# First item of the expert stage: rows fetched, copied and turned in the router's block; its bias row loaded by SyncE

## The reference, cut to what matters

```python
x = layer_norm(DEEPNORM_ALPHA * x + mix_out, ln1_g, ln1_b)
logits = x2d @ w_router + b_router
top_vals, top_idx = lax.top_k(logits, 4); gates = softmax(top_vals)
# for each expert e and its tokens:
gu = xb @ w_gate_up[e] + b_gate_up[e]          # 1024 -> 2048
hid = (clip(u, -7, 7) + 1) * (g * sigmoid(1.702 * g))   # g = min(g, 7)
y += gate * (hid @ w_down[e] + b_down[e])      # 1024 -> 1024
x = layer_norm(DEEPNORM_ALPHA * x + y, ln2_g, ln2_b)
```

## Time and profile before

| | us |
|---|---|
| median of 3 runs | 1393.29 |
| lowest, highest | 1393.19, 1395.59 |
| the profiled execution, whole | 1394.65 |
| its span | 1392.8 |
| PE busy in the span | 1342.5 (96%) |
| DVE, ACT busy | 467.6, 262.0 |
| mean granted TensorE clock | 0.978 |
| read from HBM | 493.07 MB |

### The profile page before, as it was taken

How to read it: one execution, slowest core, us unless ns; L and a number is a source line. 1 busy time by engine, 2 the same in 40 slices (tenths; PEclk the granted TensorE clock), 3 DMA queues, 4 the chain that set the end, 5 groups by cost and what they waited for, 6 DMA issues and landing times.

```text
span 1392.8 us, 20454 instructions
## 1 busy us (share of the span) xinstructions
PE 1342.5 (96%) x7640; PEld 513.0 (37%) x7641; DVE 467.6 (34%) x954; ACT 262.0 (19%) x613; POOL 78.3 (6%) x87
## 2 busy tenths in 40 slices
PE   8899999989999999999999999999999999999995
PEld 6355445654533333333333333333333233333331
DVE  0244456655732222322223222223222322322225
ACT  1333337734320100111001101001110000111002
POOL 2022235300000000000000000000000000000000
PEclk9999999979999999999999999999999899999998
DMA  9559689794368999999999996999999999999991
GB/s 357 223 195 352 238 329 392 309 363 163 121 243 356 416 417 418 418 419 418 417 417 418 418 418 242 378 419 419 418 417 417 417 366 419 420 418 418 416 416 64
DMA packets 96630, 497.91 MB, mean 357 GB/s; under 512 B 9821, under 2 KB 10205, under 8 KB 61770
## 3 DMA queue, kind: packets, MB, share of 16 engines
q1 hardware_dynamic: 84930, 429.91, 76.4%
q0 software_dynamic: 11520, 67.11, 12.3%
q10 hardware_dynamic: 136, 0.28, 0.1%
HBM read 493.07 MB, written 3.93 MB: 357 GB/s over the span
## 4 chain that ended last, share of the span: by engine, by line
PE 64%; DMA 4%; SPq 3%; DVE 1%; issue 1%; ACT 0%; ACTq 0%; DVEq 0%
PE psum L2016 29%; PE psum L2052 15%; PE psum L1986 7%; PE psum L1463 7%; DMA arena<-in_w_gate_up 4%; SPq L268 3%; PE psum L1995 2%; PE psum L1962 1%; PE psum L2040 1%; PE psum L2073 1%; DVE arena L2237 0%; DVE arena L2260 0%; PE psum L1977 0%; DVE arena L2251 0%; ACTq L2094 0%
## 5 line engine op out<-in xcount | busy, mean ns | idle before, releaser
L2016 PE MATMUL psum<-arena 128*64 128x512 f32 x2112 | 469.2, 596 | 4.9 <-DMA arena<-in_w_gate_up 2.7
L2157 DVE SCALAR_TENSOR_TENSOR arena<-psum,arena 64x512 f32<-64x512 f32 (+1 forms) x128 | 126.8, 1010 | 449.9 <-PE psum L1986 449.9
L2016 PEld LDWEIGHTS psum<-arena 128*64 128x64 f32 x2112 | 148.4, 137 | 316.4 <-issue 306.2
L2052 PE MATMUL psum<-arena 128*64 128x512 f32 x1056 | 235.4, 598 | 0.7 <-ACT arena L2119 0.7
L2052 PEld LDWEIGHTS psum<-arena 128*64 128x64 f32 x1056 | 73.2, 137 | 160.0 <-issue 133.1
L2101 ACT ACTIVATE arena<-psum 128x512 f32<-128x512 f32 x34 | 20.3, 598 | 504.1 <-PE psum L1962 504.1
L1986 PE MATMUL psum<-arena 64*128 64x512 f32 (+1 forms) x396 | 109.7, 632 | 0.9 <-ACT arena L2123 0.9
L1463 PE MATMUL psum<-arena 128*64 128x512 f32 (+1 forms) x420 | 103.0, 608 | 1.0 <-ACT arena L2101 0.7
L2189 DVE TENSOR_SCALAR arena<-psum 128x512 f32<-128x512 f32 x33 | 22.8, 692 | 239.4 <-PE psum L2016 239.4
L1193 DVE STREAM_TRANSPOSE arena<-arena 128x1024 f32<-128x1024 f32 x64 | 74.9, 1214 | 1.8 <-DVE arena L1297 1.1
L580 PE MATMUL psum<-arena 128*128 128x512 f32 x128 | 63.8, 631 | 3.7 <-DVE arena L1182 3.7
(11 more groups left out here) (252 smaller groups left out, 994.1 us busy)
## 6 DMA issues: line engine op xcount, KB each, us to landing
arena<-in_w_gate_up SPq DMA_DIRECT2D x256, 1024.0 KB, 15.7
arena<-in_w_down SPq DMA_DIRECT2D x128, 1024.0 KB, 13.0
arena<-in_w_in SPq DMA_DIRECT2D x12, 1024.0 KB, 9.7
arena<-in_w_out SPq DMA_DIRECT2D x4, 1024.0 KB, 9.7
out<-arena SPq DMA_DIRECT2D x12, 256.0 KB, 2.1
arena<-in_x_prompt SPq DMA_DIRECT2D x4, 512.0 KB, 5.1
arena<-in_b_gate_up ACTq DMA_DIRECT2D x68, 4.0 KB
arena<-in_ln_g SPq DMA_DIRECT2D x2, 512.0 KB, 5.8
```

Of the source, the lines that this page charges most:

```text
L2016: ins = nc.tensor.matmul(psum[64 * h:64 * h + 64, n, :], x_k, slot[k][:, col:col + 512], start=False, stop=(k == KD - 1))
L2052: ins = nc.tensor.matmul(psum[64 * h:64 * h + 64, 4, :], h_k, slot[s][:, col:col + 512], start=(k == 0), stop=(k == KD - 1))
L2157: ins = nc.vector.scalar_tensor_tensor(out=r, in0=psum[0:nt, banks[h]:banks[h] + at_once, :], scalar=item_gate[0:nt, b, col], in1=r, op0=A ...
```

## The change

Item 0's steps are moved from the head of the expert block to the end of the router's block. The fetch is made in three pieces in the order (2, 0, 1), the first two behind `rows_ready` 4, the third behind 6. The bias row of expert 0 is loaded by SP, behind the down weights and behind `r_ready` 6 (its place in memory is that of `x_again`, block 1). PE adds it after the last `rank` and runs four warming matmuls there, not six. `ones_rows` is set by DVE after `pick(2)`. The two warming matmuls at the head of the expert block are gone. Item 0 waits for the constant 16, and `extras` is read after item 0.

```diff
@@ router's block, SP
                     load_weights(sp, 0, s)
+                sp.wait_ge(r_ready, 6)
+                for n in range(2):
+                    sp.dma_start(bias_row[32 * n:32 * n + 1, :], a["b_gate_up"][0, 0:1, n * D:n * D + D]).then_inc(bias_loaded, 16)
@@ router's block, PE
                 ins.then_inc(ranked, 1)
-                keep_warm(6)
+                pe.wait_ge(ones_ready, 1)
+                pe.wait_ge(bias_loaded, 32)
+                add_bias()
+                keep_warm(4)
 
                 pe.wait_ge(pick_ready, 3)
+                pe.wait_ge(rows_ready, 4)
+                fetch_block(order[0], first=True, last=False)
+                fetch_block(order[1], first=False, last=False)
                 pe.wait_ge(rows_ready, 6)
-                fetch_rows(0)
+                fetch_block(order[2], first=False, last=True).then_inc(fetched, 1)
                 pe.wait_ge(col_ready, 1)
 ...
+                pe.wait_ge(xg_ready, 1)
+                turn_rows()
@@ router's block, ACT
+                act.wait_ge(fetched, 1)
+                nc.scalar.activation(xg, psum[:, 2, :], ACT.Copy).then_inc(xg_ready, 1)
+                act.wait_ge(xg_turned, 1)
+                nc.scalar.activation(xgT, psum[:, 2, :], ACT.Copy).then_inc(xg_copied, 1)
@@ router's block, DVE
                 pick(2)
+                nc.vector.memset(ones_rows, 1.0).then_inc(ones_ready, 1)
                 off_mean(2, 0)
@@ expert block, all engines
+            body(0, first=True)
             extras = eng.value_load(count_i[0:1, 0:1], min_val=0, max_val=MAX_EXTRA)
-            body(0, first=True)
@@ expert block, PE
-                warm(2)
-                turn(0)
-                pe.wait_ge(ones_ready, 1)
-                pe.wait_ge(ones_ready, 1)
-                add_bias(0)
...
-                    loaded = pe.value_load(started_i[0:1, bass.ds(t, 1)], min_val=16, max_val=16 * EXPERTS)
+                    loaded = 16 if first else pe.value_load(started_i[0:1, bass.ds(t, 1)], min_val=16, max_val=16 * EXPERTS)
@@ expert block, ACT
-                load_bias(0)
-                copy_rows(0)
-                copy_x(0)
@@ expert block, DVE
-                nc.vector.memset(ones_rows, 1.0).then_inc(ones_ready, 1)
```

More of the change, by code:

```diff
@@ L1401, in decoder_step @@
         kept_end = top[0]
+        xg = room(512)
+        xgT = room(512)
+        bias_row = room(D)
+        ones_rows = room(SLOTS)
+        item_end, top[0] = top[0], kept_end
         x_again = room(3 * D).rearrange("p (b d) -> p b d", b=3)
@@ L1437, in decoder_step @@
         ln_loaded = sem("ln_loaded")
+        bias_loaded, xg_turned, xg_copied = sem("bias_loaded"), sem("xg_turned"), sem("xg_copied")
+        bias_used, ones_ready = sem("bias_used"), sem("ones_ready")
         sel_done, pick_ready, fetched, xg_ready = sem("sel_done"), sem("pick_ready"), sem("fetched"), sem("xg_ready")
@@ L1456, in decoder_step, with fetch_block, turn_rows, add_bias @@
         PROJ_BANK = {0: 4, 1: 0}
[L1458 to L1465, removed]
+        def fetch_block(b, first, last):
+            nt = BLOCKS[b][1]
+            for h in range(2):
+                ins = nc.tensor.matmul(psum[64 * h:64 * h + 64, 2, :], pick_rows[0:nt, b, :],
+                                       x1[0:nt, b, h * 512:(h + 1) * 512], start=first, stop=last)
+            return ins
+        def turn_rows():
+            for c in range(4):
+                ins = nc.tensor.transpose(psum[:, 2, c * P:(c + 1) * P], xg[:, c * P:(c + 1) * P], ident)
+            ins.then_inc(xg_turned, 1)
+        def add_bias():
+            for h in range(2):
+                for n in range(2):
+                    ins = nc.tensor.matmul(psum[64 * h:64 * h + 64, n, :], ones_rows[32 * n:32 * n + 1, :],
+                                           bias_row[32 * n:32 * n + 1, h * 512:h * 512 + 512],
+                                           start=True, stop=False)
+            ins.then_inc(bias_used, 1)
         def rows_of_item(dve, t):
@@ L1875, in _ @@
                 links.append(link.n)
[L1878 to L1882, removed]
+        top[0] = item_end
         gate_in, up_in, sig, hid, hidT, y_rows = (room(512) for _ in range(6))
@@ L1892, in decoder_step @@
             sem("base_ready"))
-        bias_loaded, xg_turned, xg_copied = sem("bias_loaded"), sem("xg_turned"), sem("xg_copied")
-        bias_used, hid_ready, hid_turned, hid_copied, y_copied = (
-            sem("bias_used"), sem("hid_ready"), sem("hid_turned"), sem("hid_copied"), sem("y_copied"))
+        hid_ready, hid_turned, hid_copied, y_copied = (
+            sem("hid_ready"), sem("hid_turned"), sem("hid_copied"), sem("y_copied"))
         w_used = [sem(f"w_used{s}") for s in range(RING)]
-        gate_clamped, sig_ready, ones_ready, e_dve = (
-            sem("gate_clamped"), sem("sig_ready"), sem("ones_ready"), sem("e_dve"))
+        gate_clamped, sig_ready, e_dve = (
+            sem("gate_clamped"), sem("sig_ready"), sem("e_dve"))
         base_set, scatter_ready, combined, drained = (
             sem("base_set"), sem("scatter_ready"), sem("combined"), sem("drained"))
-        def warm(n):
-            for _ in range(n):
-                nc.tensor.matmul(psum[:, 7, :], ident, tab[:, 0:BANK], start=True, stop=True)
         def items(eng, body, midway=None):
+            body(0, first=True)
             extras = eng.value_load(count_i[0:1, 0:1], min_val=0, max_val=MAX_EXTRA)
-            body(0, first=True)
             if midway is None:
@@ L1960, in turn @@
                     pe.wait_ge(xg_ready, t + 1)
-                    for c in range(4):
-                        ins = nc.tensor.transpose(psum[:, 2, c * P:(c + 1) * P], xg[:, c * P:(c + 1) * P], ident)
-                    ins.then_inc(xg_turned, 1)
+                    turn_rows()
                 def fetch(t):
                     pe.wait_ge(pick_ready, 3 * t + 3)
-                    fetch_rows(t)
+                    for b in range(3):
+                        ins = fetch_block(b, first=(b == 0), last=(b == 2))
+                    ins.then_inc(fetched, 1)
                 def tables():
@@ L2035, in body @@
                     pe.wait_ge(e_dve, 2 * t + 1)
-                    add_bias(t + 1)
+                    pe.wait_ge(bias_loaded, 32 * t + 64)
+                    add_bias()
                     pe.wait_ge(xg_ready, t + 3)
```

## The result

| | before | changed |
|---|---|---|
| median, 12 runs each, us | 1394.13 | 1397.10 |
| lowest, highest | 1389.69, 1395.59 | 1391.92, 1398.44 |
| profiled execution, span | 1392.8 | 1393.6 |
| last rank to item 0's first gate/up matmul | 18.07 | 20.50 |

The ratio is 1.0022, 95% interval 1.0012 to 1.0032: slower by 0.22%.

What follows compares the result with a forecast made beforehand. TensorE bounds the end nearly everywhere, and both chains hang on item 0's start. A start 2.4 us later plus 0.6 for the clock gave +3.0, so 1396.3 us on the median of 1393.29, range 1392.4 to 1399.0.

Steps and rivals of the forecast that it cites:

- The bias load waits behind 4 MB: SP's queue in the router's block: bias loads land behind the four down loads, at 380.5.
- the nearest row: Earlier trace's 32 KB lambda rows, issued by SP behind the input weights: 24.6 us to landing, so small loads don't pass.
- PE idles, and what stands behind the wait is late: PE after the last rank: idle 374.3 to 380.5, with bias matmuls, warming and fetch behind the wait.
- Bias, warming and fetch at half clock: PE from 380.5: `add_bias` 2.1, warming and fetch 6.3, half clock for 4.6 adding 2.3; fetch done at 391.2.
- The 2.5 us behind the fetch: Copies, turn and block change behind the fetch, all on the path; item 0 starts at 393.7, 2.4 later.
- The clock at the head: PE nearly idle from 391.2 to 393.7: a clock fall costing 1.64, given 6 in 10, so 1.0.
- the old fall in item 0's second half: Half clock in item 0's down matmuls before: may move away with the shift, 1.64 at 1 in 4, so -0.4.
- Costs of nothing: Late `extras` read, `ones_rows` memset, DVE's and ACT's other head work, SP's two issues: zero, each could cost up to 0.5.
- One to one to the end: From item 0's start to the kernel's end: any shift of that start passes to the end one to one.
- Rival 1: Bias load passes the weights, landing by 374.3: item 0 starts at 387.0, -4.3; time 1390.0; chance 0.15.
- Rival 2: Bias load waits, but its queue share empties early, near 378: item 0 starts at 391.2, time 1394.0; chance 0.09.
- Rival 3: Load waits and clock stays low through the fetch and twice in item 0, another 1.6 to 3: 1398.8; chance 0.06.

Runs made afterwards that it cites:

- e1: Changed kernel with SP issuing the two bias loads ahead of the four down-weight loads; ratio 0.9961 to the kernel before, interval 14.04 us.
- e8: Changed kernel with the two bias loads issued on ACT's queue, not SP's; ratio 0.9968 to the kernel before, interval 15.90 us.
- e9: Changed kernel with the bias loads on SP behind two of the four down loads (2 MB); ratio 0.9977 to the kernel before, interval 15.99 us.
- e2: Changed kernel with PE's bias wait and bias matmuls moved behind the turn of item 0's rows; ratio 0.9957 to the kernel before, interval 13.18 us.
- e3: Kernel before plus only a PE wait for the last down-weight load, ahead of the six warming matmuls; ratio 1.0031, interval 22.94 us.
- e4: Changed kernel, unedited, run again on a second chip; ratio 1.0005 to the kernel before, interval 19.77 us.
- e10: e1 with three warming matmuls, not four; ratio 0.9959 to the kernel before, interval 13.24 us.
- e5: Kernel before with only the constant load count 16 and `extras` read behind item 0; ratio 0.9995, interval 17.44 us.
- e11: e10 plus one warming matmul ahead of the copied-rows wait and one behind the turn; ratio 0.9971 to the kernel before, interval 13.76 us.

## Why the prediction was right, step by step

- *The bias load waits behind 4 MB.* Taken at 380.5, measured 380.64 in a block that began 0.39 late. Shown by e1, e8 and e9. Choosing the nearest row, the 24.6 us of the earlier trace rows, over the 1.9 above it is what gave the sign. The figure of 2.0 us plus bytes that the prediction takes from Anatomy of one DMA in the Trainium skill's DMA: Bandwidth & Descriptors is given there for loads issued by GpSimd. SP's 64 KB on an empty queue come near it (1.9 measured, 2.15 by it as an estimate); the bias load, with 4 MB ahead, took 10.6 us from the start of its issue to PE's release.
- *PE idles, and what stands behind the wait is late.* 6.06 of gap against 6.2. e2 and e3 show that the place on PE's queue makes the cost, 6.6 us of the interval between e4 and e2.
- *Bias, warming and fetch at half clock.* To 391.2 forecast, about 391.5 measured. `add_bias` took 1.9, not 2.1; half clock lasted some 5 us from the first warming matmul (4.6 taken) and 3.5 in e4. Right in size, and it varies by run.
- *The 2.5 us behind the fetch.* 391.5 to 394.16 is 2.7. Item 0's start: 2.82 later, of which 0.39 was there at the last rank, so 2.43 against 2.4.
- *The clock at the head.* It fell, at 1.70 (7.07 against 5.37), as given 6 in 10; the old fall in item 0's second half went, at 1.57. Together +0.1 in this execution, where I had +0.6. Both vary from profile to profile: e10 has neither fall, e2 has both. Over all twelve profiles the clock fell at the head in five of the eight that have the emptied head without warming in it, and in none of the other four (before, e3, e5, e11). That leans towards the emptied head as the cause; with so few it is not shown.
- *Costs of nothing.* The memset took 0.11 and rank and DVE followed as before; the late `extras` read leaves no gap (429.40 follows 422.31 + 7.09), and none stands behind item 0 in e5 either (426.55 follows 417.76 + 8.78).
- *One to one to the end.* Right up to item 11, then only in part in the profiled execution. By the item at 869.18 (866.87 before) the shift is 2.31: 0.6 was given back in the stretch that transfers bound. The midway bias products (L2073 before, L2085 after) then took 6.92, not 8.26, and the item after them 6.69, not 6.86; that is 1.5 from a clock that fell at about 1103.7 before and 1107.7 after. The products there took 6.74 to 8.62 over the twelve profiles, in no order that follows the change. 0.8 is left. Over 12 runs each the medians differ by 2.97, which is the forecast's 3.0. So close a match is luck: the profiled execution had 2.4 at item 0's start, 0.1 and not 0.6 from the clock there, and lost most of it again later, and no run shows how the 2.97 of the medians is made up. What gave back the 0.6 was not tried.
- *The rivals.* Rival 1's arithmetic was sound for a load that comes in time: it gave item 0 4.3 earlier, and e1 shows 4.0. Its point of decision, a landing before about 375, is borne out only roughly: in e8 and e9 PE was released 1.8 and 2.0 us after the rank's start, which in the trace of before would be about 375.2, and the interval gained 2.2 and 2.1, half of rival 1's 4.3. Rival 2 did not occur. Rival 3 did not occur as a whole: no fetch ran at half clock, but e2, e8 and e9 had its two falls in item 0. Rival 2's parts give 1393.8 and not 1394.0, and the chances add up to 0.50 slower and 0.36 no change, not 0.51 and 0.35.

## What to carry to other kernels

A small load issued behind large ones on one queue landed after all of them, here behind 2 MB as behind 4 MB; issue it first, or on another engine's queue, and look at what was issued just before it and not at its size. A wait belongs as far down an in-order queue as its user allows: the same late load cost 6.6 us of the interval ahead of the warming and the fetch (19.77 in e4, 13.18 in e2), and made no wait behind them. When a step moves into an earlier block, count its transfers' place in the queue there as part of the move.

## What the runs showed of the hardware that I had not expected

A 4 KB load with nothing ahead of it on ACT's queue took about 5 us while SP's 4 MB filled the 16 engines, where 64 KB on idle engines took 1.9: another queue overtakes, but not for free. And of the ten experiment profiles and the two of the comparison, the clock fell at the head of item 0 in some and not in others of the same or nearly the same code (e4 5.37, the changed kernel 7.07), so one profile doesn't price it. The interval moved by 0.7 between two profiles of one kernel (20.50 and 19.77).
